# The order of GpSimd's pooling sums and the second pair of sliding heads in a four-layer kernel

## What is computed

```
def swa_mixer(q, k, v, ...):      # 6 query heads, 2 key heads, windows of 128 tokens
    q, k = rms_norm(q), rms_norm(k)
    s = q . k * 64**-0.5 + bias, masked to the 128 latest keys
    lse = logaddexp(logsumexp(s), sink)
    o = exp(s - lse) . v

def pool_mixer(u, pool_w, pool_scale):
    cs = lax.cumsum(uf, axis=1), padded in front
    for g, w in enumerate((2, 4, 8, 16)):          # 64 channels each
        d = (c[:, 1:] - lo) / count - uf[..., sl]  # mean of the last w tokens, less the token
        outs.append(d @ pool_w[g])
    y = concatenate(outs) * pool_scale
```

## Time and profile before

| | |
|---|---|
| time, median of 3 runs | 2629.04 us (2625.93 to 2629.22) |
| the profiled execution's own time | 2628.46 us |
| its span | 2626.7 us |
| mean granted TensorE clock | 0.956 |
| busy: TensorE matmul, VectorE, GpSimd, ScalarE | 2412.6, 1561.1, 1492.4, 405.9 us |

### The profile page before, as it was taken

One profiled execution on the slowest core, in us unless ns is written; L12 is line 12 of the kernel. 1 busy time (PEld: TensorE's weight loads), 2 busy tenths in 40 slices (PEclk: granted clock), 3 DMA queues, 4 the chain that ended last, 5 costly groups with the idle time before them and its releaser, 6 DMA issues.

```text
span 2626.7 us, 28227 instructions
## 1 busy us (share of the span) xinstructions
PE 2412.6 (92%) x10786; PEld 1935.4 (74%) x10786; DVE 1561.1 (59%) x1482; ACT 405.9 (15%) x688; POOL 1492.4 (57%) x656
## 2 busy tenths in 40 slices
PE   5978899999997889999997689999999898999999
PEld 4666678888766668888876457788887775787887
DVE  7786676653578656665358667507666463771450
ACT  3222111110122311111000411001111132110000
POOL 3355566656646566665664465566654555565664
PEclk9988899999998899999998799999999988999999
DMA  3210122222311012222232112222232200222222
GB/s 137 70 56 1 64 81 96 96 87 99 110 62 55 1 64 97 96 96 82 99 123 73 40 64 96 80 96 96 96 112 80 81 17 16 81 97 95 96 96 80
DMA packets 37838, 207.86 MB, mean 79 GB/s; under 512 B 3532, under 2 KB 10316, under 8 KB 16888
## 3 DMA queue, kind: packets, MB, share of 16 engines
q1 hardware_dynamic: 37752, 206.70, 22.6%
HBM read 204.55 MB, written 2.13 MB: 79 GB/s over the span
## 4 chain that ended last, share of the span: by engine, by line
PE 47%; DVE 15%; ACT 2%; issue 2%; POOL 1%; DVEq 0%; ACTq 0%; POOLq 0%
PE ps L801 13%; PE ps L806 13%; PE ps L805 13%; DVE act L1637 3%; DVE ssq L1637 2%; DVE t L1645 2%; DVE h L1645 1%; PE ps L1162 1%; DVE nt L1645 1%; DVE nt L1637 1%; DVE t L1637 1%; ACT act L1310 1%; PE ps L1136 1%; PE ps L874 1%; DVE x L1637 1%
## 5 line engine op out<-in xcount | busy, mean ns | idle before, releaser
L627 POOL TENSOR_TENSOR wl<-raw,wh 128x2048 fp32r<-128x2048 f32 (+1 forms) x194 | 883.9, 4556 | 16.2
L625 POOL TENSOR_SCALAR wh<-raw 128x2048 fp32r<-128x2048 f32 (+1 forms) x194 | 358.3, 1847 | 855.7 <-PE ps L801 663.3
L801 PE MATMUL ps<-h,wh 128*128 128x512 f32 x1576 | 623.6, 396 | 41.7 <-DVE x L1637 11.4
L805 PE MATMUL ps<-h,wh 128*128 128x512 f32 x1576 | 618.2, 392 | 0.0
L806 PE MATMUL ps<-h,wl 128*128 128x512 f32 x1576 | 618.2, 392 | 0.0
L801 PE MATMUL ps<-act,wh 128*128 128x512 f32 x1120 | 442.4, 395 | 26.2 <-DVE x L1637 17.1
L805 PE MATMUL ps<-act,wh 128*128 128x512 f32 x1120 | 439.6, 393 | 0.0
L806 PE MATMUL ps<-act,wl 128*128 128x512 f32 x1120 | 439.4, 392 | 0.0
L801 PEld LDWEIGHTS ps<-h,wh 128*128 128x128 f32 x1576 | 298.8, 190 | 117.8 <-issue 34.3
L806 PEld LDWEIGHTS ps<-h,wl 128*128 128x128 f32 x1576 | 298.8, 190 | 63.0
L805 PEld LDWEIGHTS ps<-h,wh 128*128 128x128 f32 x1576 | 299.1, 190 | 62.0 <-issue 1.0
(11 more groups left out here) (339 smaller groups left out, 2870.6 us busy)
## 6 DMA issues: line engine op xcount, KB each, us to landing
raw<-w_gu SPq DMA_DIRECT2D x44, 1024.0 KB, 4.8
raw<-w_up SPq DMA_DIRECT2D x32, 1024.0 KB, 4.8
raw<-w_down_b SPq DMA_DIRECT2D x32, 1024.0 KB, 4.8
raw<-w_down_a SPq DMA_DIRECT2D x32, 704.0 KB, 4.1
raw<-w_in_a SPq DMA_DIRECT2D x14, 1024.0 KB, 4.9
raw<-w_in_f SPq DMA_DIRECT2D x13, 1024.0 KB, 4.9
raw<-w_in_r SPq DMA_DIRECT2D x11, 1024.0 KB, 4.9
raw<-w_out_a SPq DMA_DIRECT2D x8, 1024.0 KB, 7.7
```

Source lines behind the costliest of these rows:

```text
L625: pool.tensor_scalar(hi_s, raw[s][:, 0:n], 1.0, 1.0, ALU.mult, ALU.mult).then_inc(hi_done, 1)
L627: pool.tensor_tensor(lo_s, raw[s][:, 0:n], hi_s.bitcast(F32), ALU.subtract).then_inc(w_ready, 1)
L801: first = pe.matmul(out, w_hi, v_hi, start=start, stop=False)
L805: pe.matmul(out, w_hi, v_lo, start=False, stop=False)
```

## The change

Before, GpSimd runs: unit 0's rounding, the pooling sums, unit 1's rounding. After, it runs: unit 0's rounding, unit 1's rounding, the pooling sums. TensorE took the first pooling product at head 0 (between head 0's column scores and head 1's second rows) and the second at head 1. Now the first is at head 1, between its column scores and head 2's second rows, and the second behind those rows. VectorE empties both at head 1, where it emptied one at head 0 and one at head 1.

```diff
-            def attention(m, nxt=None, chunk_at=None, recurrence=False):
+            def attention(m, nxt=None, chunk_at=None, recurrence=False, pooling=None):
                 prep(m, 1)
+                if pooling is not None:
+                    windows(pooling)
                 for hd in range(m.heads + 2):
...
                     prep(SWA, 0)
-                    windows(l)
-                    attention(SWA, MLA, 3)
+                    attention(SWA, MLA, 3, pooling=l)
                     attention(MLA)
...
                     if hd < m.heads:
                         score_columns(hd)
-                    if m.name == "swa" and hd < 2:
-                        pooled(s_pool, hd)
+                    if m.name == "swa" and hd == 1:
+                        pooled(s_pool, 0)
                     if hd + 1 < m.heads:
                         score_rows(hd + 1, 1)
+                    if m.name == "swa" and hd == 1:
+                        pooled(s_pool, 1)
...
                     if hd + 1 < m.heads:
                         maxima(hd + 1, 1)
-                    if m.name == "swa" and hd < 2:
-                        pooled(l, hd)
+                    if m.name == "swa" and hd == 1:
+                        pooled(l, 0)
+                        pooled(l, 1)
```

## The result

The changed kernel took 2641.59 us (median of 7 runs, 2635.49 to 2645.59), the kernel before 2629.41 us beside it (7 runs, 2625.93 to 2631.38). The ratio is 1.0044, 95% interval 1.0032 to 1.0055: slower by 12.2 us, where 11.0 were forecast. The profiled execution took 2642.56 us.

A forecast was written before the change was run, and what follows sets the result against it. TensorE, 92% busy, bounds the whole; in the sliding heads engines wait in a ring. Waits of 3.5 and 4.2 us (7.7) plus 3.3 for the clock gave 11.0 on 2628.46: 2639.5 us, range 2632 to 2644.

The forecast's parts named there:

- GpSimd before the sums: Layer 0, GpSimd: idles for VectorE's product (145.6), rounds, then begins the sums at 148.0 instead of 133.88, 14.1 us later.
- The sums: GpSimd's pooling sums, layer 0: take 23.3 us (bounds 22.2 and 24.5), second half ready at 171.3.
- VectorE up to head 1: Layer 0: statistic's 8.64 us end at 156.8; head 1's maxima, beside the sums, give diagonals at about 161.5, against 161.8.
- 2.0 us nearly all given back: VectorE's 2.0 us lead, layer 0: nearly lost before TensorE sees it, as head 1's maxima lie beside the sums.
- TensorE at head 1: Layer 0: reaches the second pooling product at 168.0, waits 3.5 us until 171.5; head 3's maxima start 3.5 us later.
- The clock: TensorE behind the new wait: lower clock would cost 2.5 us more per layer; two thirds taken, 3.3 us in all.
- Where the lateness goes: Behind head 0's denominator: no room found, the pinch at 183.97 moves by as much as the 3.5 us lateness.
- The sum: Both layers: 7.7 us at full clock plus 3.3 for the clock, 11.0 us on 2628.46, giving 2639.5.
- VectorE's own moved evacuation costs nothing: VectorE at head 1: emptying the products (0.75 us) lies in idle time, behind maxima or beside TensorE's weighted sum.
- Faster: Rival: sums done when TensorE asks (168.0), only VectorE's 2.0 us shows in both layers; 2624.5 us, chance 0.06.
- Full clock: Rival: TensorE's clock stays up behind the wait for the second product; 7.7 us, 2636.2 us, chance 0.18.
- Swallowed: Rival: TensorE late by 3.5 us, but room further on keeps the pinch at 183.97; 0 to 3 us, chance 0.11.

The follow-up runs named there:

- sums_short: The whole change with most of the pooling sums left out (pooling mixer not computed): 2635.79 us against 2629.95 before, ratio 1.0019.
- half_first: The whole change, but GpSimd does the first half of the sums before the second pair's rounding: 2633.29 us against 2630.89 before, ratio 1.0007.
- second_at_2: The whole change, but the second pooling product is taken at head 2, behind its column scores: 2632.18 us against 2630.89 before, ratio 1.0005.
- products_only: Against before, only the products' new places on TensorE and VectorE; GpSimd's sums stay before the second rounding: 2636.45 us against 2630.89, ratio 1.0026.
- own_bank_products: New product places with GpSimd's old order, second product in bank 6 instead of bank 7: 3.0 us above before, ratio 1.0012.
- gpsimd_only: Against before, only GpSimd's new order; products stay at heads 0 and 1: 2644.46 us against 2630.89, ratio 1.0051.

## Why the prediction came out right, and what it missed

The forecast of 2639.5 us and the mechanism held: the sums end too late for a TensorE that takes them in written order. By its steps, with 0.2 us taken off the times (not the durations) for the later start of the stage in this execution:

- *GpSimd before the sums*: VectorE's product was expected at 145.6 and came at 145.6, the sums at 148.0 and came at 148.1.
- *The sums*: expected 23.3 us, measured 22.65, inside the bounds of 22.2 and 24.5. They ended at 170.7 instead of 171.3.
- *VectorE up to head 1*: the statistic took 7.33 us (148.22 to 155.55), not 8.64. That is the term that was sized worst. The instructions of the two engines met differently, and I had taken the old sum of durations for a new neighbourhood. The held diagonals of head 1 took 0.91 and 1.26 us, below the 1.40 I took. So the column scores came at 160.0, not 161.5. The "2.0 us nearly all given back" were in truth kept.
- *TensorE at head 1*: that and a path of 6.1 us instead of 6.5 made TensorE earlier at the second product, 166.0 instead of 168.0, and the wait 4.78 us instead of 3.5. It cost nothing more, as the end of the wait was set by GpSimd.
- *The clock*: two thirds of the lower level were assumed, 3.3 us. With the wait filled, the marker loses 2.7 us. Right in kind and nearly in size. Two thirds was a choice and not a finding, so that it came out is in part luck.
- *Where the lateness goes*: nearly unchanged to head 5, as said (41.8 and 41.8 us, against 41.8 and 41.4). The clamp that ended at 183.97 now ends at 188.5.
- *The sum*: 9.9 us at head 0's reciprocal against the 11.0 forecast for the path. The median is 12.2 above before. The two profiled executions are 14.1 us apart: 9.9 in the stage, 0.4 from head 0 to head 5, -0.8 and +3.8 in the two parts behind the stages (below), 0.8 elsewhere. No term of the sum stands for the 4 us outside the stage. That the median came within 1.2 us of the forecast's 11.0 is so in part luck: the stage gave a little less, and the rest a little more.

What the prediction missed is the bank. "VectorE's own moved evacuation costs nothing" looked at VectorE's time only and not at who waits for it. Both products share bank 7, and with the first one moved to head 1 its emptying comes behind the maxima of the second rows. That costs nothing in the change, because the sums end 1.2 us later. But the rival *Faster* was priced at 4.0 us under before for sums that are done in time. The runs with such sums and VectorE's early start are 5.8 (sums_short) and 2.4 us (half_first) above their before. Its price was wrong. Its small chance rested on the sums not being done when TensorE asks, and that held (170.7 against 166.0); the bank is a second reason, which I had not given. The rivals *Full clock* and *Swallowed* are out by the granted clock of 0.59 and by the unchanged ring.

How the loss is made up follows from the same runs: with neither wait (second_at_2) the stage is level with before; with the bank alone it is +1.8 to +6.7 of marker (sums_short, half_first, products_only); with the late sums +9.9. The 6.7 is the bank without VectorE's early start, which only GpSimd's new order brings; the 4.5 of half_first has the lower clock of one layer in it. What is left in own_bank_products, +2.6, is partly the second product's own 0.7 us in each layer; the rest I did not separate.

## What to carry to other kernels

- Moving a block of work behind an item that waits for another engine delays it by that wait and not only by the item: here 2 us of rounding pushed 22 us of sums back by 14. Look for the idle time of the engine in front of the moved item, and put as much of the block there as fits.
- When two products of one bank move together, the emptying of the first becomes a wait of the second. Ask of each moved evacuation who waits for it and what stands before it in its engine's queue.
- A wait of TensorE can be paid twice, as idle time and as clock. Here the lower level stood behind each of the unfilled waits for the sums in the traces (3.77 to 6.93 us, six in three kernels) and behind one of the six waits of 2.32 us for the bank. If a wait can't be removed, the price of the clock behind it belongs in the sum, as a bound where the level isn't known.

## What the runs showed of the hardware

How long the same instructions take on VectorE and GpSimd depends on how they meet: the same seven of the statistic took 8.64, 7.33 and 6.1 us in three orders, and the same 22 of the sums 23.5 and 22.65. A pair of 128 x 128 diagonals took 0.48 us with GpSimd idle and up to 1.59 beside the sums.

Equal work on TensorE behind the stage doesn't take equal time. From head 5's reciprocal to the statistic behind the output projection of layer 1 it took 121.4 us before and 125.3 after. Two stretches of it, before and after (length, busy, granted clock):

```profile
870.00:940.00 70.00, 62.03 (x285) 0.90 0.00 1
```

```profile
882.00:952.00 70.00, 62.72 (x278) 0.85 0.00 1
```

The granted clock is 0.90 in one and 0.85 in the other. Over all profiled kernels here but gpsimd_only this part took between 121.4 and 125.3 us in layer 1 and between 126.2 and 130.4 in layer 0, without an order that follows from the edits. It goes with the part's mean granted clock: in layer 1 five kernels took 121.4 to 121.6 us at 0.93, three 122.7 at 0.90, and three 125.2 to 125.3 at 0.89, the change among these. So a single time of this kernel can be some 4 us off in either layer with the clock of work that nobody touched, and a stage's own marker tells more than the total. What decides which clock an execution gets there is open.
